# Splitting each gate*up tile right behind its silu, and weight pieces shared out around the join

## What is computed

```python
def swiglu(h, w_gate, w_up, w_down):
    return (jax.nn.silu(h @ w_gate) * (h @ w_up)) @ w_down
# first block, layer l:
    h = rms_norm(x, ffn1_norm[l])
    x = x + 0.5 * swiglu(h, ffn1_w_gate[l], ffn1_w_up[l], ffn1_w_down[l])
    ... mixer ...
    h = rms_norm(x, ffn2_norm[l])
    x = x + 0.5 * swiglu(h, ffn2_w_gate[l], ffn2_w_up[l], ffn2_w_down[l])
# second block, layer l: the adaptive rows come from one matrix-vector product
    mod = (c_act @ w_ada[l] + b_ada[l])[:, None, :]
```

## Time and profile before

| | |
|---|---|
| runs | 1588.49, 1592.45, 1600.69 us |
| profiled execution, its own time | 1597.33 us |
| its span | 1595.5 us |
| TensorE busy | 1563.8 us, 98% of the span |
| VectorE, ScalarE busy | 1094.9 us (69%), 1008.6 us (63%) |
| mean granted TensorE clock | 0.993 of full speed |

### The profile page before, as it was taken

How to read it: one execution, slowest core, us unless ns; L and a number is a source line. 1 busy time by engine, 2 the same in 40 slices (tenths; PEclk the granted TensorE clock), 3 DMA queues, 4 the chain that set the end, 5 groups by cost and what they waited for, 6 DMA issues and landing times.

```text
span 1595.5 us, 21865 instructions
## 1 busy us (share of the span) xinstructions
PE 1563.8 (98%) x7808; PEld 1300.0 (81%) x7808; DVE 1094.9 (69%) x1884; ACT 1008.6 (63%) x1952; POOL 96.1 (6%) x155
## 2 busy tenths in 40 slices
PE   8999999999999999999999999999999999999998
PEld 6887888778888778888777888998788889878886
DVE  5586788777776667678877677767655477575554
ACT  6665577765655555468766564776665478685552
POOL 0000021000000000011110000001100010110000
PEclk9999999999999999999999999999999999999999
DMA  9899874279987899874358997642777555158761
GB/s 306 257 336 298 285 173 141 77 242 287 291 305 171 274 250 304 269 215 145 106 176 270 284 294 242 200 169 93 215 209 221 182 193 210 56 186 241 213 209 49
DMA packets 149515, 344.73 MB, mean 216 GB/s; under 512 B 66848, under 2 KB 67616, under 8 KB 148896
## 3 DMA queue, kind: packets, MB, share of 16 engines
q1 hardware_dynamic: 130416, 290.25, 57.6%
q10 hardware_dynamic: 18992, 53.09, 12.0%
HBM read 329.64 MB, written 1.06 MB: 207 GB/s over the span
## 4 chain that ended last, share of the span: by engine, by line
PE 85%; DVE 6%; DMA 4%; ACT 3%; issue 1%; POOL 1%; ACTq 0%; SPq 0%; DVEq 0%; POOLq 0%
PE PS L1041 24%; PE PS L1042 24%; PE PS L1043 24%; DMA QF<-QF 3%; PE PS L1220 2%; DVE Wl L1930 2%; PE PS L1241 2%; PE PS L1283 1%; DVE QTl L1930 1%; PE PS L1381 1%; PE PS L1382 1%; PE PS L1383 1%; DMA raw<-in_ffn 1%; PE PS L1263 1%; PE PS L1059 1%
## 5 line engine op out<-in xcount | busy, mean ns | idle before, releaser
L1930 DVE TENSOR_TENSOR Wl<-raw,Wh 128x1024 fp32r<-128x1024 f32 (+3 forms) x360 | 354.6, 1030 | 34.3 <-ACT Wh L1519 33.4
L1041 PE MATMUL PS<-Wh,Hh 128*128 128x512 f32 (+1 forms) x824 | 321.8, 390 | 2.8 <-DVE Hl L1990 2.8
L1043 PE MATMUL PS<-Wh,Hl 128*128 128x512 f32 (+1 forms) x824 | 318.9, 387 | 0.0
L1042 PE MATMUL PS<-Wl,Hh 128*128 128x512 f32 (+1 forms) x824 | 318.6, 387 | 0.0
L1519 ACT ACTIVATE Wh<-raw 128x1024 fp32r<-128x1024 f32 (+3 forms) x360 | 305.6, 899 | 18.6 <-PE PS L1043 16.8
L1930 DVE TENSOR_TENSOR QTl<-raw,QTh 128x1024 fp32r<-128x1024 f32 (+3 forms) x236 | 231.7, 1021 | 26.4 <-ACT QTh L1519 25.6
L1041 PE MATMUL PS<-QTh,Hh 128*128 128x512 f32 (+2 forms) x536 | 209.2, 390 | 0.0
L1519 ACT ACTIVATE QTh<-raw 128x1024 fp32r<-128x1024 f32 (+3 forms) x236 | 200.0, 891 | 11.8 <-PE PS L1043 10.1
L1043 PE MATMUL PS<-QTh,Hl 128*128 128x512 f32 (+2 forms) x536 | 207.2, 386 | 0.0
L1042 PE MATMUL PS<-QTl,Hh 128*128 128x512 f32 (+2 forms) x536 | 206.9, 386 | 0.0
L1604 ACT ACTIVATE WK<-PS,st 128x256 f32<-128x256 f32 x88 | 41.5, 472 | 236.3 <-PE PS L1043 236.2
(11 more groups left out here) (239 smaller groups left out, 2329.5 us busy)
## 6 DMA issues: line engine op xcount, KB each, us to landing
raw<-in_ffn SPq DMA_DIRECT2D x392, 512.0 KB, 5.5
BT<-in_ada ACTq DMA_DIRECT2D x96, 512.0 KB, 4.9
raw<-in_win SPq DMA_DIRECT2D x64, 512.0 KB, 4.8
raw<-in_wo SPq DMA_DIRECT2D x32, 512.0 KB, 5.4
raw<-in_win SPq DMA_DIRECT2D x8, 420.0 KB, 4.5
raw<-in_lat SPq DMA_DIRECT2D x6, 512.0 KB, 5.9
raw<-in_ffn SPq DMA_DIRECT2D x8, 256.0 KB, 6.0
BT<-in_nab SPq DMA_DIRECT2D x2, 1024.0 KB, 7.9
```

The source lines that it names most:

```text
L1041: e.matmul(out_, xh, wh, start=start, stop=False)
L1042: e.matmul(out_, xh, wl, start=False, stop=False)
L1043: return e.matmul(out_, xl, wh, start=False, stop=stop)
L1930: ins = e.tensor_tensor(low(p)[:, cc], raw[p % RAW][:, cc], high(p)[:, cc].bitcast(f32), ALU.subtract)
```

## The change

Two things change, both in the order of instructions. No instruction is added or dropped.

`with_packs` puts a tile's pack directly behind its silu, ahead of the next event. And the pieces of weights are no longer all taken at the `gu` events: a `gu` event from `gu 1 1` to `gu 8 1` may take two pieces on ScalarE and one on VectorE, and a `turn` event of groups 0 to 7 two on ScalarE and three on VectorE (none before).

```diff
 def with_packs(ev):
-    out, due = [], None
+    out = []
     for e in ev:
         out.append(e)
-        if due:
-            out.append(due)
-            due = None
         if e[0] == "gu" and by_dma(e[1]):
-            due = ("pack", e[1], e[2], 0)
+            out.append(("pack", e[1], e[2], 0))
     return out
...
-        def room(ev):
+        def room(ev, ahead):
             what, g, t, z = ev
+            if what == "gu" and (1, 0) < (g, t) < (NG - 2, 0):
+                return ahead
+            if what == "turn" and by_dma(g):
+                return 4 - ahead
             if what == "down":
...
-                        goal = (0, 12, 16, 16, 16, 18)[at] if s == 0 and at < 6 else n if laid else n + 2 * room(ev)
+                        goal = (0, 12, 16, 16, 16, 18)[at] if s == 0 and at < 6 else n if laid else n + 2 * room(ev, ahead)
...
-        act_weights, dve_weights = weights_to(ACT_WALK), weights_to(DVE_WALK)
+        act_weights, dve_weights = weights_to(ACT_WALK, 2), weights_to(DVE_WALK, 1)
```

More of the change, by code:

```diff
@@ L580, in room, with weights_to @@
             return {"gu": 4}.get(what, 0)
-        def weights_to(order):
+        def weights_to(order, ahead):
             to, n = {}, 0
```

## The result

The changed kernel takes 1651.36 us (median of 4 runs, 1649.76 to 1654.14) where the kernel before took 1596.57 on the same chip: ratio 1.035, interval 1.029 to 1.040, **slower by 3.5%**. Forecast were 1642 (1604 to 1662). The profiled execution took 1654.14 us, 56.8 above that of before; its span is 1652.3 and its mean granted clock 0.982 (0.993 before). One execution of the kernel before, 2580.88 us beside e1 to e4, is left out of the ratios as a slow one.

What follows compares the result with a forecast made beforehand. TensorE, busy in all but 31.7 us, bounds the kernel. Terms for starts, packs and rounds, less waits won, sum to +50: 1647 on the profiled 1597.3, which stands 4.9 above the median, so 1642 us, range 1604 to 1662.

Steps and rivals of the forecast that it cites:

- start of FFN 4, FFN 5, each: TensorE waits 1.7 before down 0 0 and 5.0 before down 0 1, in place of 0.23; with clock +8.7 us each.
- start of FFN 1: Waits of 1.8 and 6.2 us before the first two downs, in place of 0.97; with 2.2 of clock +9.3.
- start of FFN 3: Same as at the start of FFN 1: +9.3 us.
- start of FFN 2: Waits of 8.1 us and 2.2 of clock, less 4.1 for a wait and its clock already there: +6.2.
- start of FFN 0: down 0 0 stays; down 0 1 is late by what a join and a piece add: +2.6 us.
- pack ahead of the next event: Pack in front of events TensorE waits for: 1.4 us in FFNs 4 and 5 each, 0.9 in FFN 2; +3.7.
- rounds of FFN 0: Rounds with ada steps take 17.6 us against TensorE's 16.3; five rounds lose 1.3 each, less 0.85: +5.6.
- rounds of FFNs 1 to 3: Rounds take 16.7 us, so 0.4 x 6 less 0.85 is lost in each; +4.2 for three.
- won in mid-FFN: Waits for Wl at 133.54 and 597.64 go with their clock: -4.35 and -4.2 us.
- The chain: From a product's start through pack, pieces, join and subtraction to TensorE at FFN starts: 6.7 us.
- The rule on short waits: Skill's warning that recurring short waits restart the array slow; for all new waits it would add 8 us, some 1650.
- Rival A: Chain short at FFN starts, waits for QTl and Wl go: faster, 1569 to 1576 us; chance 0.07.

Runs made afterwards that it cites:

- e1: Changed kernel's new place of the pack, with pieces divided as in the kernel before; 1624.36 us, ratio 1.019 to the kernel before.
- e4: Changed kernel with the change only from group 2 on, packs and order before that as in the kernel before; 1620.93 us, ratio 1.018 to the kernel before.
- e3: Changed kernel, but VectorE takes its pieces as before, all at the gu events; 1709.27 us, ratio 1.073 to the kernel before.
- e7: Changed kernel, but VectorE takes two pieces at gu and two at turn; 1624.45 us, ratio 1.018 to the kernel before.
- e2: Changed kernel's new division of pieces, with packs where the kernel before had them; 1624.02 us, ratio 1.019 to the kernel before.
- e8: Changed kernel, but each ada step reduces 8 of its 1024 columns; 1639.4 us, ratio 1.025 to the kernel before.
- e10: Kernel before, with three pieces on either engine added at turn 0 0 of FFN 0; 1593.83 us, ratio 0.9986 to the kernel before.
- e6: Kernel before with only the pieces divided the new way, from gu 2 1 on, all packs in their old place; 1592.74 us, ratio 0.9967 to the kernel before.
- e9: e6 with three pieces on either engine added at turn 0 0 of FFN 0; 1589.89 us, ratio 0.9956 to the kernel before.

## Why the prediction was right

The time lies inside the forecast range, the chance of 0.66 lay on the mechanism that came, and its terms can be set against the rows. Measured is the difference in waits, and for the clock a stretch's time less 0.227 us for each matmul in it.

| term | forecast | measured |
|---|---|---|
| start of FFN 4, FFN 5, each | 8.7 | 1.71 + 4.64 - 0.23 + 2.6 = 8.7 |
| start of FFN 1 | 9.3 | 6.18 - 0.97 + 1.8 + 2.6 = 9.6 |
| start of FFN 3 | 9.3 | 7.78 - 0.97 + 1.3 = 8.1 |
| start of FFN 2 | 6.2 | 7.78 - 2.51 + 1.6 - 1.5 = 5.4 |
| start of FFN 0 | 2.6 | 9.41 - 5.18 + 1.1 = 5.3 |
| pack ahead of the next event | 3.7 | 2 x 1.39 + 0.87 + 2.6 = 6.3 |
| rounds of FFN 0 | 5.6 | 4.3 for AT, 2.0 for pieces = 6.3 |
| rounds of FFNs 1 to 3 | 4.2 | 1.5 |
| won in mid-FFN | -8.6 | -8.3 |
| sum | +50 | +52 |

The starts of FFNs 1 to 5, on which the forecast rested, measure 40.5 for 42.2. That the sums agree within 2 us is partly luck: the misses are 6.6 us upwards and 4.7 downwards. Of the 9 us between 1642 and the 1651 measured, 4 are the median of the kernel before, which came out at 1596.57 and not at 1592.45.

- **The chain** of 6.7 us is 6.70 in FFN 4 (1168.69 to 1175.39) and 6.75 in FFN 2. That its end, and not VectorE's order by itself, decides is shown by e3 and e7.
- **Mis-sized: the start of FFN 0.** I counted the join and a piece alone (which are 1.12 + 1.14 = 2.3, not the 2.6 that I wrote). The pack of `gu 0 0` now stands also ahead of the squares of the second token tile, waits there for its product, and the next silu, at 24.82, is late. ScalarE:

```profile
20.35 0.45 ACT L1605 ACTIVATE WK<-PS,st 128x256 f32<-128x256 f32 x1
22.13 0.62 ACT L1619 COPY QF<-WK 128x512 uint16<-128x512 uint16 x1 [1.33 <-DVE WK L2021]
...
24.82 0.47 ACT L1605 ACTIVATE WK<-PS,st 128x256 f32<-128x256 f32 x1 [1.01 <-POOL st L2455]
```

  The kernel before had that silu at 22.77; TensorE now waits 2.34 at 25.87. e1, which has the pack's place alone, has the same wait (2.33), e2 has not.
- **Mis-sized: the pack's clock.** The waits of 2.79 for `Hl` came as forecast (2.8); that a drop of clock would follow I had left to the range, and it did, 1.2 and 1.4 us.
- **Mis-sized: the rounds of FFNs 1 to 3**, 0.5 us in each in place of 1.4. The `ada` steps' part in them is shown by e8; the 0.85 us of tolerance that I took off had no row behind it.
- **Two readings of the rows before were wrong.** I wrote that no wait up to 1.40 us was followed by half clock. One of 1.20 in the mixer was, at 787.35 (its stretch is shown in the last section). And the waits at 133.54 and 597.64 do not lie at an FFN's start but in its middle. The first is a reason why I gave the first waits of the starts no loss of clock; one of the five was followed by 1.8 us of it.
- **The rule on short waits.** Of the five first waits of 1.71 to 1.87 one was followed by half clock, so the 8 us that I worked out beside the rule of the Trainium skill ("TensorE: Matmul & The Clock Gate", "HAM oscillation — how this bites in real kernels") did not come. I had stretched that rule: the waits that the section describes are some 3 to 5 us long and come with every tile. The one drop of clock cost nothing in the end: `down 0 0` took 4.6 us (358.26 to 362.88) in place of 3.0 in FFN 2 (554.88 to 557.89), and the wait behind it was 4.32 in place of 5.92, since the subtraction came by its own chain: from the one `down` to the other it is 8.94 us in FFN 1 and 8.93 in FFN 2.
- **Left open:** 5 of the 57 us. Waits and stretches above add up to 52; the rest is in TensorE's busy time (+16.8, of which the stretches give 12), and was not followed. Open too is how much of the -8.3 is the change's: the wait of 2.56 at 597.64, 4.2 with its clock, is also absent in e1 and e10, whose pieces are divided as before.
- **Rival A** (pieces ahead of the join save the waits for pieces) was right in that waits for `Wl` go, and e6, where the starts are left alone, is 4 us faster. Of its 10.5 us of waits the 5.18 near 35 became 3.73 and 3.34 for the subtraction. Its condition, a second subtraction within 2.72 us of the first, failed: in FFN 4 TensorE goes on behind the two 7.66 us apart (1175.39 to 1183.05).

## What to carry to other kernels

Work of a steady rate (here pieces of weights) that is put ahead of a link in a chain is free only as long as that chain has slack for all of it, on every engine that it crosses: add up product to consumer through both queues, and compare it with the cover at the tightest place, not in the average round. The tightest place here is where the pipeline fills, `down 0 0` and `down 0 1` with 2.72 us between them. The same pieces did no harm where the engine waited for a DMA anyway, and shortened a wait there (e9). And a rule that changes in mid-stream needs its seam counted: an allowance made smaller before its complement begins starves the next consumer (e4).

## What the runs showed of the hardware

- A wait of the same length need not have the same consequence for the clock: 1.86 us at 358.26 was followed by a granted 0.62 over 4.5 us, 1.86 at 554.88 by 1.00. The wait of 1.20 in the mixer, which both kernels have twice, was followed by 0.63 at 788 and 1.00 at 291 before, and by 0.75 at 299 and 1.00 at 812 after:

```profile
788.00:791.60 3.60, 3.60 (x15) 2.56 (x12) 3.57 (x9) 3.35 (x10) 0.00 (x0) 0.63 0.63 204
```

```profile
299.30:303.00 3.70, 3.69 (x16) 2.87 (x17) 3.67 (x10) 2.93 (x9) 0.00 (x0) 0.75 0.62 188
812.00:816.00 4.00, 3.77 (x20) 2.99 (x21) 3.97 (x10) 3.23 (x10) 0.00 (x0) 1.00 0.58 179
```

  The first fence is the kernel before, the second the changed one.
- The same holds above 2.5 us. e1 waits 2.70 before `down 0 1` in FFN 4 and 2.71 in FFN 5; full clock followed the first, half clock the second:

```profile
1158.90:1161.90 3.00, 3.00 (x13) 2.45 (x14) 1.96 (x3) 2.97 (x5) 0.00 (x0) 1.00 1.00 255
1457.90:1460.90 3.00, 3.00 (x8) 2.35 (x8) 2.07 (x3) 3.00 (x4) 0.00 (x0) 0.50 0.98 272
```

- The part of a slow stretch that falls into a wait is not paid. In the changed kernel's wait of 5.92, which ended at 563.81, the granted clock was 0.50 for the last 3.2 us, and 1.6 us were lost behind it; in that of 4.64, which ended at 1183.05, for the last 1.1 us or so, and 2.6 were lost:

```profile
560.60:563.80 3.20, 0.00 (x0) 0.00 (x0) 2.57 (x4) 3.14 (x6) 0.00 (x0) 0.50 1.02 253
1181.90:1183.00 1.10, 0.00 (x0) 0.00 (x0) 1.10 (x3) 1.10 (x2) 0.00 (x0) 0.50 0.84 302
```
